# Four token mixers beside their gate products: the output weights of branches A, D and C as high and low parts

## The reference

```python
gates = jax.nn.sigmoid(z_gate.astype(jnp.float32)).astype(h.dtype).reshape(bsz, seq, N_BRANCHES, D_MODEL)
merged = jnp.zeros((bsz, seq, D_MODEL), h.dtype)
for n, o in enumerate((o_a, o_b, o_c, o_d)):
    merged = merged + gates[:, :, n] * (o.reshape(bsz, seq, BRANCH_WIDTH) @ w_branch[n])
return merged @ w_out
```

## Time and profile before

| what | us |
|---|---|
| median of three runs (lowest to highest) | 1894.32 (1893.85 to 1895.16) |
| profiled execution, device time | 1896.61 |
| its span, first to last instruction | 1894.7 |
| PE busy in it | 1856.2 (98%) |
| DVE busy | 1439.2 (76%) |
| ACT busy | 1185.6 (63%) |
| the fills, layer 0 (133 to 270) and layer 1 (715 to 852) | 137 each |

### The profile page before, as it was taken

The page is one execution under the profiler, slowest core; times in us unless marked ns, Lnnn a source line. Parts: engine busy times, 40 slices in busy tenths (PEclk is TensorE's granted clock), DMA queues, the critical chain, the costliest instruction groups (busy, mean ns, idle before and its releaser), DMA issues.

```text
span 1894.7 us, 25249 instructions
## 1 busy us (share of the span) xinstructions
PE 1856.2 (98%) x9124; PEld 1510.7 (80%) x9124; DVE 1439.2 (76%) x1531; ACT 1185.6 (63%) x1184; POOL 85.6 (5%) x138
## 2 busy tenths in 40 slices
PE   7999999999999999999999999999999999999996
PEld 6877777888887987777888888888888888888875
DVE  5578566666657667665888888888888888888886
ACT  4565554444445556555777777777777777777763
POOL 3101001000001100001000000000000000000011
PEclk9999999999999999999999999999999999999998
DMA  9557456555554633446999999999999999999991
GB/s 297 182 165 237 153 183 200 200 199 187 177 205 163 203 124 123 132 145 251 339 376 367 386 370 388 383 368 393 370 389 382 367 382 370 389 383 372 388 374 60
DMA packets 242865, 526.88 MB, mean 278 GB/s; under 512 B 9088, under 2 KB 58400, under 8 KB 242672
## 3 DMA queue, kind: packets, MB, share of 16 engines
q1 hardware_dynamic: 234432, 497.65, 73.6%
q0 software_dynamic: 6208, 20.50, 3.2%
q10 hardware_dynamic: 2160, 7.87, 1.0%
HBM read 510.26 MB, written 15.73 MB: 278 GB/s over the span
## 4 chain that ended last, share of the span: by engine, by line
PE 91%; DVE 3%; DMA 2%; ACT 2%; issue 1%; POOL 0%; SPq 0%; DVEq 0%; POOLq 0%; ACTq 0%
PE ps L1391 30%; PE ps L1333 19%; PE ps L1167 9%; PE ps L1290 6%; PE ps L1155 4%; PE ps L1555 4%; PE ps L1126 4%; PE ps L1186 3%; PE ps L1292 3%; DMA ring<-in_moe_w_down_dram 1%; PE ps L1245 1%; PE ps L1363 1%; PE ps L1266 1%; PE ps L1586 1%; DMA x<-in_x_dram 1%
## 5 line engine op out<-in xcount | busy, mean ns | idle before, releaser
L2506 DVE TENSOR_TENSOR ring_lo<-ring,up_gate_hi_w 128x2048 fp32r<-128x2048 f32 x222 | 499.8, 2288 | 24.1 <-ACT up_gate_hi_w L1868 23.4
L1868 ACT CAST up_gate_hi_w<-ring 128x2048 fp32r<-128x2048 f32 x224 | 426.6, 1916 | 101.8 <-DMA ring<-in_moe_w_gate_dram 67.5
L1391 PE MATMUL ps<-up_gate_hi_w,tokens_hi 128*128 128x512 f32 x896 | 354.8, 396 | 0.2 <-DVE tokens_lo L2529 0.2
L1391 PE MATMUL ps<-up_gate_hi_w,tokens_lo 128*128 128x512 f32 x896 | 350.1, 391 | 0.0
L1391 PE MATMUL ps<-ring_lo,tokens_hi 128*128 128x512 f32 x888 | 346.3, 390 | 0.0
L1871 ACT CAST down_hi_w<-ring 128x2048 fp32r<-128x2048 f32 x112 | 213.5, 1914 | 69.2 <-DMA ring<-in_moe_w_down_dram 63.7
L2511 DVE TENSOR_TENSOR down_lo_w<-ring,down_hi_w 128x2048 fp32r<-128x2048 f32 x112 | 255.7, 2284 | 1.0 <-ACT down_hi_w L1871 1.0
L1391 PEld LDWEIGHTS ps<-up_gate_hi_w,tokens_lo 128*128 128x128 f32 x896 | 168.2, 188 | 35.8
L1391 PEld LDWEIGHTS ps<-up_gate_hi_w,tokens_hi 128*128 128x128 f32 x896 | 168.4, 188 | 33.9 <-DVE tokens_lo L2529 0.6
L1391 PEld LDWEIGHTS ps<-ring_lo,tokens_hi 128*128 128x128 f32 x888 | 167.0, 188 | 33.2
L1290 PE MATMUL ps<-hT_both,up_gate_hi_w 128*128 128x512 f32 x512 | 180.8, 398 | 0.5 <-DVE ring_lo L2469 0.5
(11 more groups left out here) (310 smaller groups left out, 2954.7 us busy)
## 6 DMA issues: line engine op xcount, KB each, us to landing
ring<-in_moe_w_gate_dram SPq DMA_DIRECT2D x112, 1024.0 KB, 5.5
ring<-in_moe_w_up_dram SPq DMA_DIRECT2D x112, 1024.0 KB, 5.8
ring<-in_moe_w_down_dram SPq DMA_DIRECT2D x112, 1024.0 KB, 8.8
ring<-in_w_in_dram SPq DMA_DIRECT2D x58, 1024.0 KB, 5.7
ring<-in_ffn_w_up_dram SPq DMA_DIRECT2D x16, 1024.0 KB, 5.4
ring<-in_ffn_w_gate_dram SPq DMA_DIRECT2D x16, 1024.0 KB, 8.0
ring<-in_ffn_w_down_dram SPq DMA_DIRECT2D x16, 1024.0 KB, 9.7
expert_slot_rows<-work POOLq DMA_DIRECT2D x17, 512.0 KB, 6.3
```

Of the source, the lines that this page charges most:

```text
L1391: m = mm(bank, xs[:, 4 * half + k, :], w[:, k, :], start=(half == k == n == 0), stop=(half == 1 and k == 3 and n == 2))
L1868: copy(up_gate_hi_w[:, j, :], ring[:, slot, :]).then_inc(run.up_gate_hi, 1)
L2506: v.tensor_tensor(expert_lo(run, b, j), ring[:, slot, :], up_gate_hi_w[:, j, :], ALU.subtract)\
```

## The change

The products with the weights of A, D and C (`SPLIT_BRANCHES`) become three rounded products. The weights of B stay plain. For each of the six groups 2 to 7, ACT copies a 128 x 1024 half of the branch weights to fp32r and DVE makes its low part; these stand in the fills of `BRANCH_SPLITS`, behind that step's gate weights. Of the mixer outputs, ACT's four copies out of `O_BANK` now give the high part, and DVE makes the low part by four subtractions of 64 x 128 from the same bank, in the next fill behind the pair's second head (`NEXT_FILL`), behind the low part of that fill's gate weights and ahead of `gate_block` of tile 1. `o_done` is now counted up by DVE for these branches. The outputs have new places (`o_parts` in the space of `oT`), and ACT's copies of D and C wait for the products that read that space before.

```diff
+SPLIT_BRANCHES = "ADC"
+BRANCH_SPLITS = {9: 2, 13: 3, 17: 4, 21: 5, 26: 6, 29: 7}
+NEXT_FILL = {n: next(m for m in range(n, len(MIXER)) if MIXER[m][0] == "fill")
+             for n, s in enumerate(MIXER) if s[0] == "pv" and s[2] in SPLIT_BRANCHES and s[3] % 2}
+LOW_OUTPUTS = {m: MIXER[n] for n, m in NEXT_FILL.items()}
...
+                if BRANCH_ORDER[order] in SPLIT_BRANCHES:
+                    pe.wait_ge(branch_split, len(BRANCH_SPLITS) * layer + group - 1)
+                    outputs = [o_parts[:, order % 2, n, :, rows] for n in range(2)]
+                    weights = branch_hi_half(group), branch_half(ring_lo, layer, group)
+                    for k in range(2):
+                        for n, (a, w) in product_parts(outputs, weights):
+                            m = mm(bank, a[:, k, :], w[:, k, :], start=(k == n == 0), stop=(k == 1 and n == 2))
+                    return m
...
+            def branch_his(layer, group):
...
+                copy(branch_hi_half(group), branch_half(ring, layer, group)).then_inc(branch_hi, 1)
...
+                        if order > 1:
+                            act.wait_ge(late_up, GROUPS * layer + 2 * (order - 1))
...
+                        ins.then_inc(o_hi if b in SPLIT_BRANCHES else o_done, 1)
...
+                        if u in BRANCH_SPLITS:
+                            branch_his(layer, BRANCH_SPLITS[u])
                         if u in MERGED_TURNS:
...
+            def branch_los(layer, group):
+
+                dve.wait_ge(branch_hi, len(BRANCH_SPLITS) * layer + group - 1)
+                v.tensor_tensor(branch_half(ring_lo, layer, group), branch_half(ring, layer, group), branch_hi_half(group),
+                                ALU.subtract).then_inc(branch_split, 1)
+
+            def output_los(layer, b, h):
...
+                dve.wait_ge(o_hi, pair_number(layer, b, h) + 1)
+                hi, lo = output_parts(b, h)
+                for hh in range(2):
+                    part = slice(hh * HD, (hh + 1) * HD)
+                    for t in range(NT):
+                        rows = slice(t * P, (t + 1) * P)
+                        ins = v.tensor_tensor(lo[part, rows], O_BANK[t * HD:(t + 1) * HD, hh, :], hi[part, rows], ALU.subtract)
+                ins.then_inc(o_done, 1)
...
-                        if u % GROUP == 0 and u:
+                        if u % GROUP == 0 and u and step_number not in LOW_OUTPUTS:
                             gate_block(layer, u // GROUP - 1, 1)
                         if u % 2 == 0 and u + 2 < UNITS or u + 2 in LATE_ODD:
                             stream_los(layer, len(NARROW_Z) + u + 2)
+                        if step_number in LOW_OUTPUTS:
+                            output_los(layer, *LOW_OUTPUTS[step_number][2:])
+                            if u % GROUP == 0 and u:
+                                gate_block(layer, u // GROUP - 1, 1)
+                        if u in BRANCH_SPLITS:
+                            branch_los(layer, BRANCH_SPLITS[u])
```

More of the change, by code:

```diff
@@ L532, in trunk @@
         oT = take(NK * SEQ)
+        o_parts = nc.alloc_sbuf_tensor_at("o_parts", [P, 2, 2, 2, SEQ], F32R, offset=work_at + 4 * 15424)
+        branch_hi_w = nc.alloc_sbuf_tensor_at("branch_hi_w", [P, 2, 2, 512], F32R, offset=work_at + 4 * 7488)
+        last_branch_hi_w = nc.alloc_sbuf_tensor_at("last_branch_hi_w", [P, 2, 2, 512], F32R, offset=work_at + 4 * 17472)
         post_tmp = oT.rearrange("p (t d) -> p t d", t=NT)
@@ L656, in trunk @@
         pv_done, o_done = sem("pv_done"), sem("o_emptied")
+        o_hi, branch_hi, branch_split = sem("o_hi_ready"), sem("branch_weight_hi_ready"), sem("branch_weight_split")
         unit_ready, gate_done, late_up = sem("unit_ready"), sem("gate_block_ready"), sem("second_tile_up_ready")
@@ L759, in gate_hi, with branch_half, branch_hi_half, output_parts @@
             return gate_hi_b if u % 2 else gate_hi_low
+        def branch_half(weights, layer, group):
+            order, blk = divmod(group, 2)
+            pos = WHERE[(layer, "branch", BRANCH_ID[BRANCH_ORDER[order]])]
+            return weights[:, pos % RING, :].rearrange("p (k c) -> p k c", k=2)[:, :, blk * 512:(blk + 1) * 512]
+        def branch_hi_half(group):
+            return (last_branch_hi_w if group >= 6 else branch_hi_w)[:, group % 2, :, :]
+        def output_parts(b, h):
+            return [o_parts[:, BRANCH_ORDER.index(b) % 2, n, h // 2, :] for n in range(2)]
+        def pair_number(layer, b, h):
+            return 2 * len(SPLIT_BRANCHES) * layer + 2 * SPLIT_BRANCHES.index(b) + h // 2
         def released(pos):
@@ L1182, in up_part @@
                 pe.wait_ge(o_done, len(JOBS) // 2 * layer + 2 * (order + 1))
-                wb = slot_of(pos).rearrange("p (k c) -> p k c", k=2)
-                bank = ps[:, 3 if last else UP, :]
+                bank, rows = ps[:, 3 if last else UP, :], slice(t * P, (t + 1) * P)
+                if BRANCH_ORDER[order] in SPLIT_BRANCHES:
[6 more added lines that the diff above has]
+                    return m
+                wb = branch_half(ring, layer, group)
                 for k in range(2):
-                    m = mm(bank, oT[:, 2 * branch + k, t * P:(t + 1) * P], wb[:, k, blk * 512:(blk + 1) * 512],
-                           start=(k == 0), stop=(k == 1))
+                    m = mm(bank, oT[:, 4 * (order % 2) + k, rows], wb[:, k, :], start=(k == 0), stop=(k == 1))
                 return m
@@ L1797, in stream_his @@
                     copy(gate_hi(u), stream_full(layer, n)).then_inc(stream_hi, 1)
+            def branch_his(layer, group):
+                if group < 4:
+                    act.wait_ge(scored, SETS * layer + SET0[8])
+                elif group < 6:
+                    act.wait_ge(late_up, GROUPS * layer + group - 1)
+                else:
+                    act.wait_ge(scored, SETS * (layer + 1))
+                loaded(act, WHERE[(layer, "branch", BRANCH_ID[BRANCH_ORDER[group // 2]])])
+                copy(branch_hi_half(group), branch_half(ring, layer, group)).then_inc(branch_hi, 1)
             def weight_his(layer, kind, i):
@@ L2076, in _ @@
                         _, j, b, h = s
+                        order = BRANCH_ORDER.index(b)
+                        if order > 1:
+                            act.wait_ge(late_up, GROUPS * layer + 2 * (order - 1))
                         act.wait_ge(pv_done, SETS * layer + SET0[j + 1])
+                        to = output_parts(b, h)[0] if b in SPLIT_BRANCHES else oT[:, 4 * (order % 2) + h // 2, :]
                         for hh in range(2):
                             for t in range(NT):
-                                ins = copy(oT[hh * HD:(hh + 1) * HD, 2 * BRANCH_ID[b] + h // 2, t * P:(t + 1) * P],
-                                           O_BANK[t * HD:(t + 1) * HD, hh, :])
-                        ins.then_inc(o_done, 1)
+                                ins = copy(to[hh * HD:(hh + 1) * HD, t * P:(t + 1) * P], O_BANK[t * HD:(t + 1) * HD, hh, :])
+                        ins.then_inc(o_hi if b in SPLIT_BRANCHES else o_done, 1)
                         if (b, h) == ("B", 3):
@@ L2774, in _ @@
                 tile_los(layer, "pre", 1)
-                for s in MIXER:
+                for step_number, s in enumerate(MIXER):
                     if s[0] == "z" and s[1] in WIDE_Z[:-1]:
```

## The result

The changed kernel takes 1903.91 us (median of 5 runs, 1901.95 to 1907.16), the kernel before, run beside it, 1895.16 (5 runs, 1893.85 to 1896.47): a ratio of 1.0045 [1.0034, 1.0056], 8.75 us slower. I had forecast 1898.9 and a range to 1903: the direction was right, the size too small, the time 0.9 us outside the range.

The account below looks back on a forecast made before the run. PE was taken to bound the kernel (busy 98% of the span). Waits of 6.3 us against 3.9 of gain made each layer 2.4 slower, 4.8 in both, 1894.32 to 1899.1; forecast time 1898.9, range 1891 to 1903.

Parts of the forecast that it names:

- the gain: Branch products of A, D and C on PE: 12 a layer, each 0.34 us shorter, less 0.2: 3.9 us a layer.
- wait 1: Unit 11, head D1's softmax: PE waits for the unit's low part behind DVE's added work, 0.95 us a layer.
- wait 2: Unit 15, head D3: PE waits for the unit's low part, late in DVE's queue, 1.7 us a layer.
- wait 3: Second scores of head C3: PE waits for the mask pass, late in DVE's queue, 1.4 us a layer.
- wait 4: Group 6's product: PE waits for the low part of its branch weights, 2.25 us, in both layers.
- the four output subtractions: DVE's 64 x 128 subtractions out of the bank, per fill pair: 1.1 us taken, range 0.82 to 1.24.
- the sum: Over the fills: 6.3 us of waits against 3.9 of gain, 2.4 us slower a layer, 4.8 in both.
- The draw: Rival: DVE's queue comes out 1 us sooner at units 15 and C3's second scores; 1895.1 us, chance 0.25.
- the hidden low parts: Rival: DVE's idle time in the fills hides all low parts, 1886.5 us, or half, 1891.0; chance 0.15 together.
- The undrained queue of D: Rival: in D's heads DVE never catches up, one more wait a layer, 4.4 us in both; 1903.5, chance 0.10.

Follow-up runs that it names:

- e5: Changed kernel with only D and C split, group 5's low part in fill 18, group 6's in 25, gated sums ahead of outputs' low parts: 1891.69 us, ratio 0.9971.
- e1: Changed kernel with one number altered: the low part of group 6's branch weights in fill 25, not 26: 1897.39 us, ratio 1.0007 to the kernel before.
- e2: Kernel before plus one unused 128 x 1024 DVE subtraction that PE waits for ahead of group 6's product: 1900.83 us, ratio 1.0027.
- e8: Kernel before plus two unused 128 x 1024 DVE subtractions that PE waits for ahead of group 6's product: 1905.76 us, ratio 1.0047.
- e9: Kernel before plus unused DVE subtractions of 128 x 1024 and 128 x 256 that PE waits for ahead of group 6's product: one run, 1902.71 us beside 1898.16.
- e7: The changed kernel again, unaltered, beside the kernel before: 1904.09 us (6 runs), ratio 1.0043.
- e6: e5 with branch A split as well, so all of A, D and C, in e5's placement: 1897.12 us, ratio 0.9999 to the kernel before.
- e10: Changed kernel with only branch C split (groups 6 and 7), low parts where the change puts them: one run, 1903.41 us beside 1898.16 for the kernel before.
- e3: Changed kernel with branch C plain again, only A and D split (groups 2 to 5): 1896.99 us, ratio 1.0005 to the kernel before.

## Why the prediction came out too low

**Right: the gain.** The prediction had 12 products 0.34 us shorter, less 0.2 at the end, 3.9 a layer. Products take 1.36 to 1.39 us outside the low clock, the last transposition waits for 0.22, and e5, which has the gain without the waits, bears it out at 2.36 for eight products (2.5 expected).

**Right: four waits at the places named.** Idle and 0.27 for a restart behind a DVE low part:

| | predicted | layer 0 | layer 1 |
|---|---|---|---|
| wait 1, unit 11 | 0.95 | 1.08 | 1.08 |
| wait 2, unit 15 | 1.7 | 1.75 | 1.75 |
| wait 3, scores of C3 | 1.4 | 1.49 | 1.49 |
| wait 4, group 6's weights | 2.25 | 2.46 | 2.34 |
| sum | 6.3 | 6.78 | 6.66 |

Each was to be read off DVE's queue, not off its share: DVE stands idle for 22 to 23% of these windows now and PE waited for it all the same. e1 takes wait 4 away and leaves the other three as they were to 0.01 us, and e2 makes it alone.

**Too small: the four output subtractions at 1.1 us.** DVE's timeline of after:

```profile
163.32 1.22 DVE L2377 TENSOR_TENSOR ring_lo<-ring,gate_hi_low 128x1024 fp32r<-128x1024 f32 x1
164.46 1.19 DVE L2395 TENSOR_TENSOR o_parts<-ps,o_parts 64x128 fp32r<-64x128 f32 x4
165.68 0.69 DVE L2363 SCALAR_TENSOR_TENSOR xn<-egate,ps 128x512 f32<-128x512 f32 x1
166.28 1.22 DVE L2383 TENSOR_TENSOR ring_lo<-ring,branch_hi_w 128x1024 fp32r<-128x1024 f32 x1
167.41 0.42 DVE L2507 CUSTOM_DVE_ANT_0 work<-ps,cn 128x256 f32<-128x256 f32 x1
```

In a queue a piece costs what it holds off the next one, from start to start. The low part of unit 10 costs 1.14 (163.32 to 164.46) and that of the branch weights 1.13 (166.28 to 167.41), as assumed. The four subtractions cost 165.68 - 164.46 = 1.22 us, not 1.1: they are near the upper end of the range, 1.24. The group lasts 1.19, and one of them 0.29 (286 ns is the mean of the 48), so they start 0.30 apart. By the Trainium skill, VectorE: DVE Perf Modes, "Two Vector instructions with no wait between them", an instruction whose input or output begins in another quarter of the partitions than the last one's is held until all before it are finished. By that rule, the trace agrees: 0.30 from start to start is the length of one, and the four stand where the prediction said the rule would put them.

**Wrong: the sum stood for a PE at full clock.** The step that failed is "Sum. 0.95 + 1.7 + 1.4 + 2.25 = 6.3 us of waits against 3.9 of gain". It priced wait 4 by its idle time and a restart, and put what follows the wait at nothing without a reason. Behind it, in layer 0, the clock falls to 1.2 GHz for 3.4 us. From group 6's product to the turn layer 0 takes 1.24 us more than layer 1, though layer 1 has in that stretch a wait of 0.3 that layer 0 lacks (below): the fall costs 1.5 us. e1 without the wait has no fall in the fills, e8 and e9 with a longer one have it in both layers, e2 with 2.07 and 2.10 in neither. The prediction says nothing of the clock, and nothing of the idle time of before could have told it: there PE never stood still in these stretches.

**Too small by a little: the waits themselves.** Waits 1 to 4 were 0.05 to 0.2 longer than I had them (0.4 a layer in sum). The four subtractions explain the first three: 0.12 more in each makes 1.07, 1.82 and 1.52, against 1.08, 1.75 and 1.49 measured, so the prediction's own upper value for them was the better one. There is also a fifth wait that I did not name: unit 30's low part, behind the gated sum of group 7, is late by some hundredths, and its 12 matmuls take 3.02 us instead of 2.77. It is in e1 and e5 too. It costs 0.3 us, in layer 1 alone in after. In layer 0 the 12 matmuls take 2.77; as I read it, the low clock brought PE to them later and so gave DVE the time.

**The account:** 4.8 predicted + 1.5 (clock, layer 0) + 0.8 (waits 1 to 4 longer) + 0.3 (unit 30) = 7.4, and the fills of both layers grew by 4.29 + 2.97 = 7.26. The medians of the five runs differ by 8.75. The remaining 1.5 is not settled: it is within what executions of one kernel differ by, and e7, with six runs, has 1904.09 against 1896.66, 7.4 us (here the medians of each kernel's runs).

**Rivals.** The draw and the hidden low parts fall with the four waits. The undrained queue of D would have given about my measured time, 1903.5, and for the wrong reason: there is no further wait in D, and head C0 starts without one. A time that fits is no proof of its mechanism. In e6, where the order is another, a piece of that rival does appear (the row at 789.80).

**Still open:** why the clock falls behind wait 4 in layer 0 and not in layer 1. It fell behind 2.19, 2.14 and 2.09 us of idle, all in layer 0, and not behind 2.07 (e2, layer 0), nor behind 2.01, 2.07, 2.10 and 2.12, all in layer 1; behind 2.38, 3.15 and 3.33 it fell wherever it was tried. The lengths overlap, so something else has a say. The windows show that the fall is not timed by the wait. It begins 1.3 us behind the wait's end in after, at its end in e10 (253.6, by the mean of 0.91), and in e9's layer 0 0.1 us ahead of it (252.6 against 252.74, by the mean of 0.66), while PE still stands. So a rival to something that sets layer 0 apart is that the moment at which a wait near 2.1 us happens to lie decides, differently from one execution to the next. No run varied the moment alone, and each kernel has one profiled execution, the changed one two.

## What to carry to other kernels

Price work that is added to a half-idle engine at the places where another engine waits for it, as a queue with a start, its members and a deadline; a load ahead in that queue is part of it, and a one-line move to the other side of that load won back most of what this change lost. Count each member of the queue from its start to the next one's start. Take a stall of a saturated PE of some 2 us or more at more than its idle time: ask what the clock does behind it. And where a change has parts that are alike (three branches), the ones whose deadlines have room can be kept alone: D and C gave 5.0 us, with A as well nothing.

## What the runs showed of the hardware

- In e9 an idle of 2.38 us on a PE that had been busy throughout the fills until then went with 3.4 us at 1.2 GHz, in both layers; the low clock cost 1.5 to 1.6 us. One of 1.49 us never did, nor e3's of 1.65; idles of 2.0 to 2.2 us did in three of eight cases.
- A 1 MB weight load landed 5.0 us after its issue in after and more than 7 in e3, in the same place of the program, and a wait of 1.65 us came from that alone.
- PE's restart behind a wait for DVE costs 0.2 to 0.3 us (2.24 and 2.37 us of longer fills for 2.07 and 2.10 of idle in e2).
- Four DVE subtractions of 64 x 128 out of PSUM, between halves of the partitions, start 0.30 us apart and hold off the next instruction for 1.22 us.
